# Seven block products in place of eight for six of the eight ungated column groups of one feed-forward matrix

## The reference, cut to what matters

```python
def conv_ffn(h, w_up, conv_w, conv_b, w_down):     # h: 512 x 1024, normalised
    z = h @ w_up                                   # w_up: 1024 x 4096
    u = z[..., :D_FF]                              # D_FF = 2048: the ungated half
    g = dwconv3_centred(z[..., D_FF:], conv_w) + conv_b
    return (jax.nn.gelu(g, approximate=False) * u) @ w_down
```

## Time and profile before

| | |
|---|---|
| time, median of 3 runs | 2225.1 us (2225.05 to 2225.28) |
| the profiled execution's own time | 2225.39 us |
| its span, first to last instruction | 2223.6 us |
| PE busy | 2205.6 us, 99% |
| DVE / ACT / POOL busy | 987.8 / 873.5 / 1008.9 us |
| phase `up1` on PE | 927.5 to 1102.2 us |

### The profile page before, as it was taken

The page is one execution under the profiler, slowest core; times in us unless marked ns, Lnnn a source line. Parts: engine busy times, 40 slices in busy tenths (PEclk is TensorE's granted clock), DMA queues, the critical chain, the costliest instruction groups (busy, mean ns, idle before and its releaser), DMA issues.

```text
span 2223.6 us, 25953 instructions
## 1 busy us (share of the span) xinstructions
PE 2205.6 (99%) x11052; PEld 1844.3 (83%) x11052; DVE 987.8 (44%) x1192; ACT 873.5 (39%) x1076; POOL 1008.9 (45%) x431
## 2 busy tenths in 40 slices
PE   9999999999999999999999999999999999999998
PEld 7888888888888888888888888878878888888887
DVE  6252335342143405253413645278587234666603
ACT  4254434232321444332334426265564534322312
POOL 5527334444445472355443642434333453554443
PEclk9999999999999999999999999999999999999999
DMA  6315223323333351333333431343241333333222
GB/s 234 104 57 171 76 69 100 98 95 95 96 99 99 106 159 48 95 97 102 95 108 101 142 86 58 106 124 98 67 116 39 95 133 95 95 99 99 97 95 76
DMA packets 161379, 223.67 MB, mean 101 GB/s; under 512 B 24288, under 2 KB 87776, under 8 KB 161008
## 3 DMA queue, kind: packets, MB, share of 16 engines
q1 hardware_dynamic: 159424, 216.87, 31.4%
q10 hardware_dynamic: 1840, 5.15, 0.7%
HBM read 215.13 MB, written 6.85 MB: 100 GB/s over the span
## 4 chain that ended last, share of the span: by engine, by line
PE 94%; DVE 3%; ACT 1%; DMA 1%; issue 0%; POOL 0%; ACTq 0%; DVEq 0%; SPq 0%
PE ps L1259 82%; PE ps L1483 2%; PE ps L1480 1%; PE ps L1515 1%; PE ps L1345 1%; PE ps L1676 1%; PE ps L1495 1%; PE ps L1616 0%; PE ps L1332 0%; PE ps L1505 0%; PE ps L1691 0%; PE ps L1703 0%; PE ps L1684 0%; PE ps L1382 0%; PE ps L1718 0%
## 5 line engine op out<-in xcount | busy, mean ns | idle before, releaser
L610 POOL TENSOR_TENSOR w_lo<-w_raw,w_hi 128x1024 fp32r<-128x1024 f32 x377 | 963.7, 2566 | 1169.6 <-ACT w_hi L697 1154.9
L697 ACT ACTIVATE w_hi<-w_raw 128x1024 fp32r<-128x1024 f32 x378 | 396.1, 1057 | 873.7 <-DMA w_raw<-w_in 133.8
L1259 PE MATMUL ps<-XH,w_hi 128*128 128x512 f32 x1760 | 688.2, 391 | 0.2 <-ACT TC L1058 0.2
L1259 PE MATMUL ps<-XH,w_lo 128*128 128x512 f32 x1760 | 685.1, 389 | 0.0
L1259 PE MATMUL ps<-XL,w_hi 128*128 128x512 f32 x1760 | 684.8, 389 | 0.0
L1259 PE MATMUL ps<-HID,w_hi 128*128 128x512 f32 x1728 | 532.2, 389 | 0.1
L1259 PEld LDWEIGHTS ps<-XH,w_hi 128*128 128x128 f32 x1760 | 330.4, 188 | 70.3 <-issue 1.0
L1259 PEld LDWEIGHTS ps<-XH,w_lo 128*128 128x128 f32 x1760 | 330.3, 188 | 68.9
L1259 PEld LDWEIGHTS ps<-XL,w_hi 128*128 128x128 f32 x1760 | 330.4, 188 | 68.7 <-issue 1.0
L1259 PEld LDWEIGHTS ps<-HID,w_hi 128*128 128x128 f32 x1728 | 324.2, 188 | 67.6 <-DVE HID L2739 0.5
L1259 PE MATMUL ps<-HID,w_lo 128*128 128x512 f32 x864 | 336.1, 389 | 0.0
(11 more groups left out here) (426 smaller groups left out, 2314.5 us busy)
## 6 DMA issues: line engine op xcount, KB each, us to landing
w_raw<-w_in SPq DMA_DIRECT2D x72, 512.0 KB, 3.7
w_raw<-ffn_w_up SPq DMA_DIRECT2D x128, 256.0 KB, 2.8
w_raw<-w_up SPq DMA_DIRECT2D x88, 256.0 KB, 3.1
w_raw<-xa_wkv SPq DMA_DIRECT2D x32, 512.0 KB, 3.7
w_raw<-ffn_w_down SPq DMA_DIRECT2D x32, 512.0 KB, 3.8
w_raw<-w_in_c SPq DMA_DIRECT2D x24, 512.0 KB, 3.8
w_raw<-w_down SPq DMA_DIRECT2D x22, 512.0 KB, 3.6
w_raw<-xa_wq SPq DMA_DIRECT2D x16, 512.0 KB, 3.8
```

The source lines that it names most:

```text
L610: nc.gpsimd.tensor_tensor(w_lo[:, s, :, :], w_raw[:, s, :, :], w_hi[:, s, :, :].bitcast(F32), ALU.subtract).then_inc(lo_done, 1)
L697: nc.scalar.activation(w_hi[:, s, :, :], w_raw[:, s, :, :], ACT.Copy).then_inc(hi_done, 1)
L1259: mm = nc.tensor.matmul(ps[:, bank + m, :], a, b, start=start and j == 0 and n == 0, stop=stop and j == 1 and n == 2)
```

## The change

In `up1`, groups 1 to 6 (`FAST`) are computed in another way; groups 0 and 7 stay as they are. For one such group:

- **Units.** Each unit now holds 4 feature tiles x 256 columns of one half (ungated or gated), loaded by one DMA of 512 KB, in place of 2 feature tiles x 512 columns in two DMAs. Units 0 and 1 of a group are ungated, 2 and 3 gated.
- **Gated units** (`deep_products`): the same 24 matmuls of 128 x 512 a unit, in another order.
- **Ungated units** (`fast_products`): the weights in a pair of feature tiles and the two column tiles are 2 x 2 blocks, the inputs 2 x 2 blocks of a feature tile and 256 tokens. Seven block products (Strassen's scheme in a form with shared sums) take the place of eight: 42 matmuls of 128 x 256 a unit. Four of the seven take blocks as loaded (`plain`), three take sums of weight blocks (`summed`).
- **Sums of weights** (`fast_weights`): DVE makes four sums of 128 x 256 for each ungated unit, each waiting for the one before it, in `FWS` and in place in `w_raw`. ACT splits the unit only after them and also makes their high part `FWH` (128 x 768); POOL makes the low part `FWL` (128 x 768) behind `w_lo`.
- **Sums of inputs**, once: ACT makes four `FXB` (128 x 256), DVE sixteen sums of 128 x 256 (`fast_inputs`), ACT four `FXH` and DVE four `FXL` (128 x 1024 each).
- **Sums of results** (`fast_sums`): ACT copies one half bank to `UU`, DVE does five additions that read PSUM and write `UU`. Then `UU = UU * R`, with both inputs in SBUF, is the first step of `group`.
- **Order.** Fast groups use banks 4 to 7 for the block products and 0, 1 or 2, 3 for the gated tiles. PE waits for all `FXL` before group 1, for the `fast_sums` of group g - 1 before group g, and for `GP` of group g - 2 before the gated tiles. ACT, in this layer, splits the first unit of the group after next behind the `HID` copy. DVE's order is: `fast_weights` for the second ungated unit of group g + 1, `fast_sums(g)`, `group(g)`, with `fast_weights` for the first ungated unit of group g + 2 in it between the convolution and `HF`.

```diff
+        FAST = range(1, FF1 // 256 - 1)
...
+                        if u in deep:
+                            kt, c = deep[u]
+                            sp.wait_ge(w_used, u - RING + 1)
+                            sp.dma_start(by_kt(w_raw, u % RING),
+                                         mat.rearrange("(k p) n -> p k n", p=P)[:, kt:kt + 4, c:c + 256]
+                                         ).then_inc(w_loaded[u % RING], 16)
...
+                    pool.wait_ge(na_and_fw_hi, FW0 + i + 1)
+                    nc.gpsimd.tensor_tensor(FWL[:, i % 2], FWS[:, i % 2], FWH[:, i % 2].bitcast(F32),
+                                            ALU.subtract).then_inc(b2_and_fw_lo, 1)
...
+                    act.wait_ge(na_and_fw_sum, FW0 + 4 * fast_unit[u] + 4)
                 nc.scalar.activation(w_hi[:, s, :, :], w_raw[:, s, :, :], ACT.Copy).then_inc(hi_done, 1)
+                if u in fast_unit:
+                    i = fast_unit[u] % 2
+                    nc.scalar.activation(FWH[:, i], FWS[:, i], ACT.Copy).then_inc(na_and_fw_hi, 1)
...
-                    split_to(first[name] + (1 if name.startswith("up") else 3) + LEAD)
+                    split_to(first[name] + {"up0": 1, "up1": 0, "up2": 1}.get(name, 3) + LEAD)
...
+                    fast = l == 1 and g in FAST
+                    if fast:
+                        act.wait_ge(w_used, u0 + 4 * g + 2)
+                        nc.scalar.activation(UU[:, 1, HT:T], ps[:, 6, 0:HT], ACT.Copy).then_inc(f2_and_fx_act, 1)
                     split_to(u0 + 4 * g + 4 + LEAD)
...
-                    split_to(u0 + 4 * g + 5 + LEAD)
+                    if l == 0:
+                        split_to(u0 + 4 * g + 5 + LEAD)
                     act.wait_ge(ffn_dve, g * FD + nd + 9)
                     nc.scalar.activation(HID[:, 2 * g:2 * g + 2, :], HF[:, :, :], ACT.Copy).then_inc(ffn_act, 1)
+                    if l == 1:
+                        split_to(u0 + 4 * g + 5 + LEAD)
...
+                    pe.wait_ge(f2_and_fx_dve, FX_LO + KT // 2)
+                    for g in FAST:
+                        pe.wait_ge(f2_and_fx_dve, FC0 + 5 * (g - FAST[0]))
+                        for h in range(2):
+                            fast_products(u0 + 4 * g + h, h, 4)
+                        pe.wait_ge(ffn_dve, nd + (8 if g < 3 else FD * (g - 2) + 2))
+                        for h in range(2):
+                            deep_products(u0 + 4 * g + 2 + h, h, 2 - 2 * (g % 2))
+                    pe.wait_ge(f2_and_fx_dve, FC0 + 5 * len(FAST))
+                    group(u0 + 4 * (ng - 1), 4, 4, XH, XL)
...
+                    nc.vector.tensor_tensor(FWS[:, h, 1], a11, a21, ALU.subtract).then_inc(na_and_fw_sum, 1)
+                    dve.wait_ge(na_and_fw_sum, FW0 + 4 * i + 1)
+                    nc.vector.tensor_tensor(a21, a21, a22, ALU.add).then_inc(na_and_fw_sum, 1)
+                    dve.wait_ge(na_and_fw_sum, FW0 + 4 * i + 2)
+                    nc.vector.tensor_tensor(FWS[:, h, 0], a21, a11, ALU.subtract).then_inc(na_and_fw_sum, 1)
+                    dve.wait_ge(na_and_fw_sum, FW0 + 4 * i + 3)
+                    nc.vector.tensor_tensor(FWS[:, h, 2], a12, FWS[:, h, 0], ALU.subtract).then_inc(na_and_fw_sum, 1)
...
+                    dve.wait_ge(f2_and_fx_act, FX_FIRST + g - FAST[0] + 1)
+                    nc.vector.tensor_tensor(quarter[:, 0:2], pair(4), over(quarter[:, 3], 2), ALU.add).then_inc(f2_and_fx_dve, 1)
+                    dve.wait_ge(f2_and_fx_dve, FC0 + n + 1)
+                    nc.vector.tensor_tensor(quarter[:, 2], quarter[:, 1], ps[:, 7, 0:HT], ALU.add).then_inc(f2_and_fx_dve, 1)
+                    dve.wait_ge(f2_and_fx_dve, FC0 + n + 2)
+                    nc.vector.tensor_tensor(quarter[:, 3], quarter[:, 2], ps[:, 6, HT:T], ALU.add).then_inc(f2_and_fx_dve, 1)
+                    nc.vector.tensor_tensor(quarter[:, 1], quarter[:, 1], ps[:, 6, HT:T], ALU.add).then_inc(f2_and_fx_dve, 1)
+                    dve.wait_ge(f2_and_fx_dve, FC0 + n + 4)
+                    nc.vector.tensor_tensor(quarter[:, 1:3], quarter[:, 1:3], pair(5), ALU.add).then_inc(f2_and_fx_dve, 1)
+                    dve.wait_ge(f2_and_fx_dve, FC0 + n + 5)
+
...
+                fast_inputs()
+                fast_weights(0)
+                fast_inputs_lo()
+                fast_weights(1)
                 dve.wait_ge(r_done, norm_of[name] + 1)
                 for g in range(ng):
-                    group(g, 4 * (g % 2))
+                    ahead = 2 * (g + 2 - FAST[0])
+                    ahead = ahead if ahead < 2 * len(FAST) else None
+                    if g in FAST:
+                        if g + 1 in FAST:
+                            fast_weights(2 * (g + 1 - FAST[0]) + 1)
+                        fast_sums(g)
+                        group(g, -2 * (g % 2), True, ahead)
```

More of the change, by code:

```diff
@@ L1280, in group, with deep_products @@
                         after()
+            def deep_products(u, h, bank):
+                hi, lo = by_block(w_hi, u % RING), by_block(w_lo, u % RING)
+                pe.wait_ge(lo_done, u + 1)
+                for m in range(2):
+                    for j in range(4):
+                        kt = 4 * h + j
+                        for n in range(3):
+                            wt = (lo if n == 2 else hi)[:, j // 2, j % 2, m, :]
+                            mm = nc.tensor.matmul(ps[:, bank + m, :], wt, (XL if n == 1 else XH)[:, kt, :],
+                                                  start=kt == 0 and n == 0, stop=kt == KT - 1 and n == 2)
+                mm.then_inc(w_used, 1)
@@ new lines, in fast_products, with block, sums, tile @@
+            def fast_products(u, h, bank):
+                i = fast_unit[u]
+                hi, lo = by_block(w_hi, u % RING), by_block(w_lo, u % RING)
+                first_half, second_half = slice(0, HT), slice(HT, T)
+                def block(m, j):
+                    return lambda p: [w[:, p - 2 * h, j, m, :] for w in (hi, lo)]
+                def sums(s):
+                    return lambda p: [w[:, i % 2, s, p - 2 * h, :] for w in (FWH, FWL)]
+                def tile(j, cols):
+                    return lambda p: [x[:, 2 * p + j, cols] for x in (XH, XL)]
+                def mixed(t):
+                    return lambda p: [x[:, p, t, :] for x in (FXH, FXL)]
+                plain = ((block(0, 0), tile(0, first_half), 2, 0), (block(0, 1), tile(1, first_half), 0, 0),
+                         (block(1, 1), mixed(3), 1, 1), (block(1, 0), mixed(0), 2, 1))
+                summed = ((sums(2), tile(1, second_half), 1, 0), (sums(0), mixed(1), 0, 1), (sums(1), mixed(2), 3, 0))
+                opens, closes = ((2, 0), (0, 0), (1, 1), (3, 0)), ((2, 1), (0, 1), (1, 0), (3, 0))
+                for part in (plain, summed):
+                    if part is plain:
+                        pe.wait_ge(lo_done, u + 1)
+                    else:
+                        pe.wait_ge(b2_and_fw_lo, FWL0 + i + 1)
+                    for p in (2 * h, 2 * h + 1):
+                        for a, b, at_bank, side in part:
+                            (a_hi, a_lo), (b_hi, b_lo) = a(p), b(p)
+                            out_cols = ps[:, bank + at_bank, side * HT:(side + 1) * HT]
+                            nc.tensor.matmul(out_cols, a_hi, b_hi, start=p == 0 and (at_bank, side) in opens, stop=False)
+                            nc.tensor.matmul(out_cols, a_hi, b_lo, start=False, stop=False)
+                            mm = nc.tensor.matmul(out_cols, a_lo, b_hi, start=False,
+                                                  stop=p == KT // 2 - 1 and (at_bank, side) in closes)
+                mm.then_inc(w_used, 1)
@@ L2232, in step @@
                     def step(n):
-                        dve.wait_ge(ffn_dve, g * FD + (nd + n))
+                        dve.wait_ge(ffn_dve, g * FD + (nd + n + (1 if fast and n < 8 else 0)))
+                    if fast:
+                        nc.vector.tensor_tensor(UU[:, :, :], UU[:, :, :], over(R[:, :], 2), ALU.mult).then_inc(ffn_dve, 1)
                     dve.wait_ge(w_used, g * 4 + (u0 + 4))
```

135 lines of the change are left out of this document (112 added, 23 removed).

## The result

The changed kernel takes 2249.56 us (median of 4 runs, 2248.87 to 2251.7) against 2225.18 us in the same session; the ratio is 1.0111, 95% interval [1.0098, 1.0123]. It is 24.4 us slower; predicted were 29.1 us. The profiled execution took 2250.13 us, its span is 2248.3 us.

A forecast was written before the change was run, and what follows sets the result against it. PE bounds the kernel before; after, the port shared by POOL and DVE bounds `up1`. Group 2 at 986.2, plus 4 x 25.6, 20.96 and 21.76, ends `up1` at 1131.3: +29.1 us, forecast 2254, range 2239 to 2263.

The forecast's parts named there:

- PE's work: In `up1`, 84 narrower matmuls at 0.120 us replace 48 per fast group: 0.80 us saved each, 4.8 us over six.
- The port as the bound: In a fast group POOL and DVE exclude each other on one SBUF port: 23.4 us of work against PE's 20.96.
- side-by-side rival: POOL and DVE overlap, so PE waits only at the start, 4.7 us against 4.8 saved: 2225.0; chance 0.12.
- list of signs: What the later profile would show: PE waits of about 4 to 5 us in `up1`, released by DVE's `fast_sums` or `UU`.
- The start: In `up1`, PE starts group 1 at 955.2, its gated tiles after 971.2 and group 2 at 986.2.
- The period: Time per fast group, groups 2 to 6: 23.4 us of port work plus 2.2 idle, 25.6 us, four times.
- Its holes: Twice a period POOL has nothing to do while DVE doesn't use the port: 1.13 us and 1.1 us.
- the queue's sum of 26.1: The period counted along the queue, from one `fast_sums` end to the next: 26.1 us; 25.6 was taken.
- Group 6: Last fast group of `up1`: starts at 1088.6, PE not stopped from there, 20.96 us.
- clock rival: Waiting drops PE to 1.2 GHz; block products take 20.2 us, gated tiles 3.5 us late: 14 us more, 2268; chance 0.08.
- The sum: Whole kernel: `up1` ends at 1131.3 instead of 1102.2, nothing given back afterwards: +29.1 us.
- Port packed: Rival: POOL's queue fills the two holes, period 23.4 or a little less, 9 us less, 2244.5; chance 0.18.

## Why the prediction was right, and where its sizes were off

- **PE's work.** Predicted 4.8 us less; with nothing else changed it is 5.2.
- **The port as the bound.** Right. The phase gets most of its time back without the weight sums (2227.2), with short POOL instructions (2224.7) and with the convolution reading PSUM (2233.2), each edit by itself. The side-by-side rival falls with the rows of 2.62 and 1.95 us for a sum that takes 0.42 alone. PE's wait before group 1 is released by POOL's `w_lo`, as in the working of the start, though the list of signs named DVE only.
- **The start.** PE was to start group 1 at 955.2, its gated tiles after 971.2 and group 2 at 986.2; measured 954.5 (behind `w_lo`), 971.35 (the end of `UU`, L2379) and 984.55. 1.65 us too much, all of it after 971: the four weight sums behind `UU` were to meet the rest of a `w_lo`, but POOL's last had ended at 969.0 and they ran free (1.1 us), and the next four were overestimated like those of the period.
- **The period** is the term that was mis-sized: 25.6 us predicted, 24.66 measured, four times, 3.8 us. Its holes were right (`HID`'s wait 1.13 us, and some 1.2 us of `fast_sums`, both while POOL is idle). Too large were the two stretches in which DVE and POOL take turns: from `GP` to the last `CV` 9.4 us in place of 10.2, and the four weight sums behind `HID` 5.5 in place of 5.95. I had taken 2.4 us for a `w_lo` from the earlier trace rows, three in 7.31 us, and added a `CV` of 0.45 to each; but one `CV` already lay in those 7.31 us (the second ended 0.3 us behind them). Two `w_lo` take 4.78 us beside a convolution in PSUM and 5.12 here with two `CV` let in, so a `CV` adds 0.17 us. The two stretches are 1.2 us shorter than in the queue's sum of 26.1, which leaves 24.9.
- **Group 6.** 20.96 us predicted, 22.6 measured from PE's start to its end (1083.2 to 1105.8): +1.6, and with the clock held up 21.0. The clock rival was right that the clock falls, not in what follows: the gated tiles were there when DVE came to them in each of groups 1 to 5, and the price was 1.6 us in place of 14. Its block product at the lower level was also too dear, 0.24 us; the trace has 0.213 (ten intervals in group 6, 1083.78 to 1085.91 us).
- **The sum**: 29.1 - 1.65 - 3.8 + 1.6 = 25.3; `GP` of the last group came 25.5 us later than before. The phases behind gave 0.8 us of it back in the profiled execution, where I had said nothing; what gave it back was not looked into.
- **Port packed.** POOL's holes come from ACT's order, as said: they are in the trace, and closing one gave 3.5 us.

The Trainium skill puts the rule that decided this case in a line, "SBUF — State Buffer", section "Summary: rules for kernel authors": where VectorE is in its two-port mode, or has two SBUF inputs while the GpSimd instruction reads SBUF, the second one to issue is blocked until the first has finished. The runs agree from both sides, 2.62 us for 0.42 with two SBUF inputs, and 2.71 us for four `CV` with one in PSUM.

The price of the cure stands in the trace as well: the first two `CV` take 0.88 us from SBUF and 1.41 from PSUM. The Trainium skill gives the reason in "VectorE: DVE Perf Modes", section "Why PSUM operands drop a tier": the fast mode for float32 with one tensor input needs both SBUF read ports. The 0.5 us a group are already taken off the 4.2 us that the six instructions save.

What stays open: that the way from group 1 to group 2 is some 5 us longer than PE needs even with the convolution in PSUM was read from the trace (weight sums and `UU` are held), not tried alone.

## What to carry to other kernels

Before work is put on VectorE beside GpSimd, add up the durations of both engines' instructions that use their common port in one period, and the times in which neither can use it; compare that sum, not each engine's busy share, with what TensorE needs. An operand left in PSUM takes an instruction out of that sum at nearly the same duration (2.71 us for 2.73, but 1.41 for 0.88 in the two first `CV`). What it gives back depends on how long the instruction was held: 16 us with the six of the convolution, 4.9 with `UU` and the low part of `HID`. Look afterwards for what is then longest, here the start and the weight sums. Replacing eight products by seven saves less than an eighth when the matmuls get narrower, so the budget for what surrounds it is small (here 5.2 us of 2225).

## What was unexpected in the hardware

- The lower clock costs little where another engine sets the pace: some 24 us at 1.2 GHz in the changed kernel and a price of 1.6 us, in the one group for which nothing else waited.
- `CV` over 511 columns with its input in PSUM and shifted by one element against its output takes 0.68 us, like 512 columns from SBUF.
- What a held instruction costs is set by POOL's instruction and hardly by its own length. Four `CV` that take 2.73 us undisturbed took 7.77 us with two `w_lo` let in, 2.5 us for each `w_lo`; a weight sum of 0.42 us took 2.62 beside a `w_lo` of 2.49 and 1.95 beside an `FWL` of 2.02.
